# A hybrid encoder trunk on one core: decay of heads 1 to 7 from spread cumulated gates, the recursion's vector work in another order, and the last head's residuals moved

## The reference

```python
g = -jnp.exp(a_log) * jax.nn.softplus(a_logit + dt_bias)
g = jnp.cumsum(g in chunks of CHUNK, axis=-1)
decay = jnp.exp(jnp.where(tri, g[..., :, None] - g[..., None, :], -jnp.inf))
lower = jnp.where(strict, jnp.einsum("bhncd,bhnkd->bhnck", k_beta, k) * decay, 0.0)
a_mat = lower + jnp.eye(CHUNK)
rhs = jnp.concatenate([v * beta[..., None], k_beta * jnp.exp(g)[..., None]], axis=-1)
sol = lax.linalg.triangular_solve(a_mat, rhs, left_side=True, lower=True, unit_diagonal=True)
attn_intra = jnp.einsum("bhncd,bhnkd->bhnck", q, k) * decay
def step(state, xs):
    v_new = u_n - jnp.einsum("bhcd,bhde->bhce", w_n, state)
    o = jnp.einsum(q_n, state) + jnp.einsum(a_n, v_new)
    state = state * jnp.exp(gl_n) + jnp.einsum(k_n, v_new)
```

## Time and profile before

| what | value |
|---|---|
| three runs | 1398.73, 1400.56, 1401.97 us; median 1400.56 us |
| profiled execution, its own time | 1400.85 us |
| its span, first to last instruction | 1399.1 us |
| granted TensorE clock, mean of the span | 0.993 |
| TensorE busy | 1358.9 us, 97% |
| VectorE busy | 793.7 us, 57% |
| ScalarE, GpSimd busy | 532.4 us (38%), 250.5 us (18%) |

### The profile page before, as it was taken

How to read it: one execution, slowest core, us unless ns; L and a number is a source line. 1 busy time by engine, 2 the same in 40 slices (tenths; PEclk the granted TensorE clock), 3 DMA queues, 4 the chain that set the end, 5 groups by cost and what they waited for, 6 DMA issues and landing times.

```text
span 1399.1 us, 18107 instructions
## 1 busy us (share of the span) xinstructions
PE 1358.9 (97%) x6594; PEld 1118.9 (80%) x6594; DVE 793.7 (57%) x1205; ACT 532.4 (38%) x901; POOL 250.5 (18%) x243
## 2 busy tenths in 40 slices
PE   7989999999899999999999999989999999999998
PEld 5778888888778888888888878668888888888877
DVE  5567787777674343343465876764433434335755
ACT  6545545443253141331334421654322323223344
POOL 3545555553031000000012110002010000000211
PEclk9999999999999999999999999999999999999998
DMA  6233332322232223222322353312232322332211
GB/s 177 66 86 86 79 79 62 85 70 71 90 106 91 90 98 113 90 90 93 104 76 89 103 123 70 82 43 94 91 101 94 107 90 90 100 104 98 89 62 60
DMA packets 168575, 125.67 MB, mean 90 GB/s; under 512 B 35873, under 2 KB 165186, under 8 KB 168514
## 3 DMA queue, kind: packets, MB, share of 16 engines
q1 hardware_dynamic: 167410, 123.01, 29.6%
q10 hardware_dynamic: 1104, 1.84, 0.5%
HBM read 116.96 MB, written 5.25 MB: 87 GB/s over the span
## 4 chain that ended last, share of the span: by engine, by line
PE 79%; DVE 11%; ACT 3%; issue 2%; DVEq 2%; DMA 1%; POOL 1%; POOLq 0%; SPq 0%; ACTq 0%
PE psum L148 22%; PE psum L150 22%; PE psum L149 22%; PE psum L898 2%; DVE wL L140 1%; PE psum L909 1%; ACT wH L132 1%; DVE bL L1408 1%; DVEq L1177 1%; DVE hT L1609 1%; DVE terms L1175 1%; DVE acc L1607 1%; PE psum L1928 1%; PE psum L912 1%; PE psum L1935 1%
## 5 line engine op out<-in xcount | busy, mean ns | idle before, releaser
L148 PE MATMUL psum<-aH,wH 128*128 128x512 f32 x896 | 360.4, 402 | 4.0 <-ACT taps L744 3.4
L150 PE MATMUL psum<-aL,wH 128*128 128x512 f32 x896 | 350.7, 391 | 0.0
L149 PE MATMUL psum<-aH,wL 128*128 128x512 f32 x896 | 349.8, 390 | 0.0
L140 DVE TENSOR_TENSOR wL<-wRaw,wH 128x2048 fp32r<-128x2048 f32 (+2 forms) x125 | 240.0, 1924 | 132.7 <-ACT wH L132 127.1
L148 PE MATMUL psum<-bH,wH 128*128 128x512 f32 x720 | 284.6, 395 | 2.3 <-DVE pleT L2054 1.6
L150 PE MATMUL psum<-bL,wH 128*128 128x512 f32 x720 | 280.9, 390 | 0.0
L132 ACT CAST wH<-wRaw 128x2048 fp32r<-128x2048 f32 (+2 forms) x109 | 197.2, 1814 | 219.9 <-PE psum L150 219.9
L149 PE MATMUL psum<-bH,wL 128*128 128x512 f32 x720 | 280.7, 390 | 0.0
L148 PEld LDWEIGHTS psum<-aH,wH 128*128 128x128 f32 x896 | 169.0, 189 | 37.6 <-ACT taps L744 3.9
L150 PEld LDWEIGHTS psum<-aL,wH 128*128 128x128 f32 x896 | 168.5, 188 | 36.1
L149 PEld LDWEIGHTS psum<-aH,wL 128*128 128x128 f32 x896 | 169.1, 189 | 32.0 <-issue 0.5
(11 more groups left out here) (295 smaller groups left out, 1503.4 us busy)
## 6 DMA issues: line engine op xcount, KB each, us to landing
wRaw<-in_mlp_w_up SPq DMA_DIRECT2D x64, 512.0 KB
wRaw<-in_mlp_w_down SPq DMA_DIRECT2D x64, 512.0 KB
wRaw<-in_dn_w_in SPq DMA_DIRECT2D x32, 512.0 KB
wRaw<-in_ple_w_gate SPq DMA_DIRECT2D x16, 512.0 KB
xScaled<-inv_blocks SPq DMA_DIRECT2D x16, 256.0 KB, 3.1
wRaw<-in_sw_w_in SPq DMA_DIRECT2D x16, 256.0 KB
wRaw<-in_sw_w_out SPq DMA_DIRECT2D x16, 256.0 KB
wRaw<-in_dn_w_out SPq DMA_DIRECT2D x8, 384.0 KB
```

The source lines that it names most:

```text
L140: last = [nc.vector.tensor_tensor(o, r, h_.bitcast(F32), ALU.subtract) for o, r, h_ in zip(*([v if half is None else v[:, half * v.shape[1 ...
L148: nc.tensor.matmul(o, wh, xh, start=first, stop=False)
L149: nc.tensor.matmul(o, wl, xh, start=False, stop=False)
L150: return nc.tensor.matmul(o, wh, xl, start=False, stop=last)
```

## The change

1. **Decay of heads 1 to 7.** The cumulated gates of all heads, which the kernel already has in PSUM, are copied to SBUF by ScalarE (`gCum`). In head 0's step TensorE turns them once, ScalarE copies the result (`gRows`), and SyncE stores it to DRAM (16 KB). For each later head SyncE loads its row of 512 values into all 128 partitions (`load_decay`, 256 KB, waiting for the exponential of the head before, since it overwrites `gA`). GpSimd subtracts the partition's own value, drains, and takes the minimum with 0; ScalarE takes the exponential from SBUF. TensorE's four matmuls remain in head 0 alone.
2. **Start of a step on TensorE.** The order decay, solve(0), gram_kk, update(0) becomes gram_kk, solve(0), update(0).
3. **Recursion on VectorE.** The second half of the panel's low part goes from behind solved(1) to behind residual(2), `blocks_inverse(4)` ahead of residual(2), and solved(2) between the halves of `blocks_inverse(8)`.
4. **Last head.** The add and the panel at the end of step 7 go into the last head's step, behind advance(0); the panel of that step is done in halves around solved(3), and tail(0) stands ahead of the add 6; the MLP's first panel is done in halves in `dn_last`; ScalarE's prep_hi stands ahead of q_part(3).

```diff
@@ gates_act3 (ScalarE), blocks_sp (SyncE) @@
             act.wait_ge(gate_cum, 1)
+            nc.scalar.copy(gCum[:].rearrange("p (h t) -> p h t", h=HEADS_A), cums[:, 0]).then_inc(gcum_ok, 1)
...
+        def load_decay(sp, h):
+            sp.dma_start(work[:, 4, :], growD.ap()[bass.ds(h, 1), :].to_broadcast([P, S])).then_inc(g_in, 16)
...
+        def blocks_sp(sp, a, more=True):
+            if isinstance(a, int) and a == 0:
+                sp.wait_ge(grow_ok, 1)
+                sp.dma_start(growD.ap().rearrange("h (t p) -> (h t) p", p=P), gRows[:]).then_inc(grow_out, 16)
+                sp.wait_ge(grow_out, 16)
+            if more:
+                sp.wait_ge(dec_ok, a + 1)
+                load_decay(sp, a + 1)
             sp.wait_ge(blk_ok, a + 1)
...
@@ g_next_dve, gA_pool @@
-            nc.vector.tensor_copy(gNext[:], gate[:, h, G_, :]).then_inc(g_ok, 1)
+            src = gate[:, h, G_, :] if isinstance(h, int) and h == 0 else gCum[:].rearrange("p (h t) -> p h t", h=HEADS_A)[:, h, :]
+            nc.vector.tensor_copy(gNext[:], src).then_inc(g_ok, 1)
...
             pool.wait_ge(g_ok, h + 1)
+            pool.wait_ge(g_in, 16 * h)
+            nc.gpsimd.tensor_tensor(gA, gA, bc(gNext[:]), ALU.subtract)
+            pool.drain()
+            nc.gpsimd.tensor_scalar(gA, gA, 0.0, None, ALU.min).then_inc(gA_ok, 1)
@@ dn_step_pe @@
-            decay()
             if b is None:
+                decay()
                 gram_kk()
                 fill(2)
                 pe.wait_ge(ss_ok, 2 * a + 2)
             else:
+                gram_kk()
                 pe.wait_ge(ss_ok, 2 * a + 2)
                 solve(0)
-                gram_kk()
                 update(0)
                 fill(2)
...
+            if b is None:
+                pe.wait_ge(gcum_ok, 1)
+                pe.wait_ge(low_ok, 1)
+                nc.tensor.transpose(bank[BZ][0:HEADS_A * NT, 0:P], gCum[:], ident[:]).then_inc(gcumT_done, 1)
@@ dn_step_act @@
-                for i in range(1, NT):
-                    q_part(i)
+                q_part(1)
+                q_part(2)
                 prep_hi(act, n, n % 2)
+                q_part(3)
...
+            else:
+                act.wait_ge(gA_ok, a + 1)
+                c_.activation(decT, gA, ACT.Exp).then_inc(dec_ok, 1)
...
+            if b is None:
+                act.wait_ge(gcumT_done, 1)
+                c_.copy(gRows[:], bank[BZ][0:HEADS_A * NT, 0:P]).then_inc(grow_ok, 1)
@@ dn_step_dve, last head @@
                 advance(0)
+                out_early_dve(dve, 4)
+                prep_lo(dve, n - 1, (n - 1) % 2)
                 for i in range(1, NT):
                     residual(i)
+                    if i == 3:
+                        prep_lo(dve, n, n % 2, 0)
                     solved(i)
                     if i == 2:
                         out_early_dve(dve, 5)
+                    if i == 3:
+                        prep_lo(dve, n, n % 2, 1)
                     advance(i)
+                tail(0)
                 out_early_dve(dve, 6)
-                prep_lo(dve, n, n % 2)
-                tail(0)
@@ dn_step_dve, recursion @@
             solved(1)
-            prep_lo(dve, n, 1, 1)
...
             blocks_inverse(2)
+            blocks_inverse(4)
             residual(2)
-            blocks_inverse(4)
+            prep_lo(dve, n, 1, 1)
...
-            solved(2)
...
-            blocks_inverse(8)
+            blocks_inverse(8, (0,))
+            solved(2)
+            blocks_inverse(8, (1,))
             blocks_out()
             advance(2)
...
-            if p is None:
-                out_early_dve(dve, 4)
-                prep_lo(dve, n + 2, 1)
@@ dn_last_dve @@
-            prep_lo(dve, N_MLP0, N_MLP0 % 2)
...
+                if m in (1, 3):
+                    prep_lo(dve, N_MLP0, N_MLP0 % 2, m // 2)
```

More of the change, by code:

```diff
@@ L436, in hybrid_trunk @@
         gateT_ok = sem("gateT_ok")
+        gcum_ok = sem("gcum_ok")
+        gcumT_done = sem("gcumT_done")
+        grow_ok = sem("grow_ok")
+        grow_out = sem("grow_out")
+        g_in = sem("g_in")
+        gCum = sbd("gCum", [P, HEADS_A * NT])
+        gRows = sbd("gRows", [HEADS_A * NT, P])
+        growD = nc.dram_tensor("decay_rows", [HEADS_A, S], F32, kind="Internal")
         logits = bank[6][:, 0:NT * GATE_COLS].rearrange("p (t c) -> p t c", t=NT)
@@ L635, in lower_sp @@
             sp.dma_start(lowBlk[0:NB, 0:B16 * B16].rearrange("b (r c) -> b r c", c=B16), diagonal(lo)[:, 0]).then_inc(low_in, 16)
-        def blocks_sp(sp, a):
+        def blocks_sp(sp, a, more=True):
[6 more added lines that the diff above has]
+                load_decay(sp, a + 1)
             sp.wait_ge(blk_ok, a + 1)
@@ L654, in dn_sp @@
             load_panel(sp, 2, 0)
-            with sp.Fori(0, HEADS_A - 3) as a:
+            blocks_sp(sp, 0)
+            load_panel(sp, 2, 1)
+            load_panel(sp, 3, 0)
+            lower_sp(sp, 1)
+            with sp.Fori(1, HEADS_A - 3) as a:
                 blocks_sp(sp, a)
@@ L667, in dn_sp @@
             lower_sp(sp, HEADS_A - 1)
-            blocks_sp(sp, HEADS_A - 1)
+            blocks_sp(sp, HEADS_A - 1, False)
             dn_out_load(sp, 3)
@@ L795, in g_next_dve @@
         def g_next_dve(dve, h):
-            nc.vector.tensor_copy(gNext[:], gate[:, h, G_, :]).then_inc(g_ok, 1)
+            src = gate[:, h, G_, :] if isinstance(h, int) and h == 0 else gCum[:].rearrange("p (h t) -> p h t", h=HEADS_A)[:, h, :]
+            if isinstance(h, int) and h == 1:
+                dve.wait_ge(gcum_ok, 1)
+            nc.vector.tensor_copy(gNext[:], src).then_inc(g_ok, 1)
         def gA_pool(pool, h):
             pool.wait_ge(g_ok, h + 1)
-            nc.gpsimd.tensor_tensor(gA, bm(maskLow[:]), bc(gNext[:]), ALU.mult).then_inc(gA_ok, 1)
+            if isinstance(h, int) and h == 0:
+                nc.gpsimd.tensor_tensor(gA, bm(maskLow[:]), bc(gNext[:]), ALU.mult).then_inc(gA_ok, 1)
+                return
+            pool.wait_ge(g_in, 16 * h)
+            nc.gpsimd.tensor_tensor(gA, gA, bc(gNext[:]), ALU.subtract)
+            pool.drain()
+            nc.gpsimd.tensor_scalar(gA, gA, 0.0, None, ALU.min).then_inc(gA_ok, 1)
         def per_tile(fn):
@@ L979, in dn_step_pe @@
                 lower(i)
+                if b is None and i == 1:
+                    pe.wait_ge(grow_ok, 1)
                 if i:
@@ L1027, in dn_step_act @@
                 return
-            act.wait_ge(dec_done, a + 1)
-            c_.activation(decT, t4(bank[BY]), ACT.Exp).then_inc(dec_ok, 1)
+            if b is None:
+                act.wait_ge(dec_done, 1)
+                c_.activation(decT, t4(bank[BY]), ACT.Exp).then_inc(dec_ok, 1)
+            else:
+                act.wait_ge(gA_ok, a + 1)
+                c_.activation(decT, gA, ACT.Exp).then_inc(dec_ok, 1)
             z_act(act, a)
@@ L1160, in pairs_inverse, with blocks_inverse @@
                 dve.drain()
-            def blocks_inverse(m):
+            def blocks_inverse(m, parts=(0, 1)):
                 nq = B16 // (2 * m)
@@ L1168, in blocks_inverse @@
                 first, corner, second = corners(xt, m)
-                for left, right, out_ in ((low, first, hf), (second.rearrange("p q c i -> p q i c"), hf, corner)):
+                steps = ((low, first, hf), (second.rearrange("p q c i -> p q i c"), hf, corner))
+                for left, right, out_ in (steps[i] for i in parts):
                     if m == 2:
```

## The result

The changed kernel takes 1406.09 us (median of nine runs, 1403.00 to 1410.96), the kernel before 1398.73 us in the nine runs beside it (1395.87 to 1404.22). The ratio is 1.0046, with a 95% interval from 1.0032 to 1.0059: slower by 0.46%, some 6.4 us by the ratio (the medians lie 7.4 us apart), where 1.8 us less was forecast and the range ended at 1402.8. The profiled execution has a time of 1404.79 us and a span of 1402.7 us, 3.6 us more than the one of before; it is the fourth quickest of the nine.

What follows compares the result with a forecast made beforehand. TensorE, holding 79% of the chain, was taken as the bound. Head 0 +0.2, decay -1.2, split +2.4, last head -2.2 and clock -1.0 gave -1.8 us, so a median of 1398.8 us, range 1394.6 to 1402.8.

Steps and rivals of the forecast that it cites:

- the split's price: VectorE's recursion, steps 1 to 6: update(2) later, walk(3)'s wait gone, net +0.4 us a step, +2.4 us in all.
- Rival (a): Recursion: the product of width 8 keeps ahead of GpSimd's taps, so the split pays; 3.9 us less, 1394.9; chance 0.2.
- The decay: Step starts on TensorE: removing four matmuls gains 0.29 us in steps 2, 4, 6 and 7, nothing elsewhere; -1.2 us.
- Rival (b): Step starts: the decay's 6.2 us arrive in full because vNew comes sooner; 5.0 us less, 1393.8; chance 0.07.
- rival (d): Heads' decay: the row load or GpSimd's passes delay the exponential, TensorE waits 0.5 us a head; 1402.3; chance 0.08.
- Rival (c): Longer waits in step 1, head 0 and the MLP's start bring stretches at 1.2 GHz; up to 1404.9; chance 0.10.
- Head 0: A 3.1 us wait for the low part, but lower(0) stays near 82.74; +0.2 us, from -0.6 to +1.2.
- Step 7: The last step before the last head, without projection: the recursion's new order makes about no change.
- Last head: Waits of 1.96 and 2.11 us go, smaller new ones come, including at the MLP's start; -2.2 us.
- the clock's term: Last head: the stretch at 1.2 GHz behind the 1.96 us wait goes; -1.0 us, between -1.7 and nothing.

Runs made afterwards that it cites:

- split_only: The kernel before with only the change's new order of VectorE's recursion (part 3); 1406.85 us, ratio to before 1.0046.
- half_back: The changed kernel with one line moved, the recursion's second half panel back behind solved(1); 1395.77 us, ratio to before 0.9971.
- fill_between: no_split with one unit of other TensorE work between solve(0) and update(0), and gram_kq ahead of walk(1); 1393.71 us, ratio to before 0.9957.
- no_split: The changed kernel with VectorE's recursion back in the order of before; 1398.81 us, ratio to before 0.9991.
- decay_only: The kernel before with only parts 1 and 2 of the change; 1400.66 us, ratio to before 1.0005.
- panel_first: no_split with the low part of the MLP's first panel ahead of the adds again; 1398.02 us, ratio to before 0.9984.
- head0_old: The changed kernel with only head 0's second half panel back in its old place; 1406.56 us, ratio to before 1.0045.
- pool_held: The changed kernel with GpSimd's taps of the query part held until VectorE has copied the inverse blocks out; 1408.24 us in one run, no ratio.
- last_only: The kernel before with only part 4 of the change, the last head's moves; 1398.70 us, ratio to before 0.9985.
- best_no_decay: half_back and panel_first joined, without parts 1 and 2 of the change; 1397.01 us, ratio to before 0.9979.

## Why the prediction was wrong

**The step that failed** is the split's price. The prediction took the first product of width 8 at 1.73 us, "by its row", as a length that comes with GpSimd's taps beside it, and had update(2) late by 0.96 us, net +0.4 a step. The loss there is 1.50 us in step 3 (waits of 1.23 to 1.57 in steps 1 to 6), net +1.0. Of the 0.5 us that were missing, the product makes 0.33: it has no length of its own beside GpSimd, it waits until GpSimd's tap sum is done. Its end hangs on GpSimd's start and not on its own: in the earlier trace rows it ends 0.84 us behind the tap sum's end (186.44, 185.60), after the change 0.82 behind it (189.90, 189.08). Starting it 0.23 us sooner against TensorE's update(1) brought nothing, since GpSimd was still first. The rest is some 0.2 us of small gaps between VectorE's short instructions. Over steps 1 to 6 that is 2.8 us of the ledger's 7.7; head 0 and step 7, below, are the other two terms that failed. In the runs' medians the split is the part that costs, since split_only is as slow as the whole change.

- **Rival (a)** named the right question, who comes first, and had the wrong answer for this kernel: with the half panel right before it the product starts 0.16 us behind the tap sum (187.84, 187.68), which had been waiting for the half panel to end. I had worked out 184.3 against 184.32 for these two, a coin's edge, and gave it a chance of 0.2. Between one engine first and the other there is a step of 1.06 us in the product's length (1.02, 2.08), and a forecast within 0.1 us of it is a forecast of both sides. The split did pay once the half panel was out of the way, in half_back.
- **The decay** came out as forecast in the steady steps. Step start to update(0) is 1.72 us against 2.01 in step 2 and 2.07 against 2.06 in step 3; the waits at update(0) were 0.44 in steps 2, 4, 6 and 7, 0.75 to 0.80 in steps 3 and 5 and 1.73 in step 1, where 0.6 to 0.7 was forecast with most in step 1. Rival (b) did not happen, and fill_between shows that its 5 us were lost at exactly the wait that the prediction named. TensorE never waited for the row load or for GpSimd's passes of 1.19 and 1.50 us, and only GpSimd itself waited for a row, once, in head 0 (5.71 us); rival (d) fell.
- **Rival (c)**, waits that bring 1.2 GHz, happened in part. In step 1 the wait of 1.7 us stands in every kernel with the decay change and without fill_between; it is followed by 1.2 GHz in the profiles of no_split, decay_only, panel_first and head0_old, and by none in those of the change, half_back and pool_held. Its price shows in head0_old and the change, which have the same step 1: 41.59 us with the stretch and 40.00 without. In the profile of decay_only, steps 2 to 6 together are 1.0 us shorter than before's (0.9 by the forecast), step 1 is 1.4 us longer with such a stretch, and head 0 is 1.2 us longer with another behind its wait of 2.58 us for the inverse blocks. That accounts for its missing gain in that one execution; how often the other runs had such stretches isn't recorded.
- **Head 0**: +1.80 instead of +0.2. The wait of 3.1 us came (3.83), but TensorE took 11.7 us for the 13 units behind it and not 8.9 or 10.6: the stretch at 1.2 GHz is longer than the one of before, twelve matmuls at 0.63 us instead of seven. So lower(0) began at 84.40 and not near 82.74, without waiting for the blocks: TensorE itself had become the late one, and the claim that VectorE's line sets this point either way is what failed. head0_old and half_back, where the blocks are waited for again, have lower(0) at 82.17 and 81.88. The measured +1.80 lies above the upper bound of +1.2.
- **Step 7**: "about no change" was +2.40. TensorE waits 2.34 us for the inverse blocks (1.28 before), and 1.2 GHz follows. VectorE's copy of the blocks comes 0.3 us sooner in its step than before, but the load took longer to land. The DMA issues of this stretch, after and before (KB each, us to landing):

```profile
xScaled<-inv_blocks SPq DMA_DIRECT2D x2, 256.0 KB, 4.4
```

```profile
xScaled<-inv_blocks SPq DMA_DIRECT2D x2, 256.0 KB, 3.2
```

  I didn't price this wait at all, although the view of TensorE's waits of before has it beside head 0's. The slower load goes with the decay part of the change: in step 7 it landed after 3.7 to 4.8 us in all ten profiles of kernels with that part, and after 3.0 to 3.2 us in all four without it (before, split_only, last_only, best_no_decay); in every other step it took 3.0 to 3.3 in all fourteen. The wait was 0.92 to 2.90 us with it and 0.96 to 1.28 without. No row load is under way in step 7, and what in the decay part makes this load slower stays open.
- **Last head**: the waits of 1.96 and 2.11 went, solve(1) waits 1.07 (1.2 forecast) and update(3) 0.20 (0.4), and no 1.2 GHz follows. But split_only and decay_only still have the wait for vNew of 1.97 and 1.98 us there, and no 1.2 GHz behind it, so the clock's term of -1.0 took for a fixed cost what the profile before happened to have. At the MLP's start the waits are 2.13 and 0.53, against 1.26 before: 1.4 more, where the text's own figures (1.7 against 1.3) gave 0.4 and its sum 0.6. Term -2.56 for -3.2; the runs of last_only say -2.1 us.

## What to carry to other kernels

In these traces VectorE's and GpSimd's instructions with two inputs in SBUF exclude each other. When such an instruction of VectorE is on the critical path, have it start clearly ahead of GpSimd's next one, don't put another one of that kind right before it, and don't price it by its recorded duration in another order, since that duration holds a wait. When work is taken off the bounding engine between two dependent steps, put other ready work there in the same edit, or the gap turns into a wait. And price every row of the waits of the bounding engine in every stage, those of a transfer too. Before a profile is taken to show what an edit did to one stage, look for a second kernel with the same instructions in that stage: head 0 of half_back and of head0_old differ by 1.9 us, nearly all of it at the clock behind one wait.

## What was not expected of the hardware

- A two-input VectorE instruction of 1.02 us beside a two-input GpSimd instruction of 1.29 us: one keeps its own time, and the other ends 0.80 to 0.84 us (VectorE's) or 1.10 to 1.12 us (GpSimd's) behind the first one's end. With starts 0.03 us apart that makes 2.08 or 2.16 us, and both outcomes stand in one execution (split_only, above).
- The same wait of 1.7 us in the same place of the program is followed by 1.2 GHz in some executions and not in others. In no_split:

```profile
98.56 0.70 PE L894 MATMUL psum<-vNew,trig 128*128 128x128 f32 x2 [1.72 <-DVE vNew L1123]
...
99.91 0.63 PE L149 MATMUL psum<-aH,wL 128*128 128x512 f32 x1
...
101.62 0.62 PE L150 MATMUL psum<-aL,wH 128*128 128x512 f32 x1
```

  against durations of 0.39 to 0.49 behind 99.37 in the change. The spread of the runs goes with the clock: among the nine runs of the change, 1403.3 us goes with a mean granted clock of 0.998 and 1411.0 with 0.988. A gain of 1 us is not seen in single runs.
- A load of 256 KB from DRAM landed after 3.2 us in the profile before and after 4.4 us in the one after, at the same place of the program, and the fourteen profiles tie it to an edit that issues no transfer in that step.
